# Two transformer blocks in one kernel: where the activation halves begin in SBUF, and the order of the first weight split

## The reference

```python
# block 1
h = rms_norm(x, g); proj = h @ w_in                  # 1024 -> 5120
o = stick_breaking_attention(q, k, v)                # 8 heads of 64
y_conv = (cb * causal_dwconv(cc * cx)) @ w_conv_branch
merged = sigmoid(g_att) * (o @ w_att_branch) + sigmoid(g_conv) * y_conv
x = x + rms_norm(merged @ w_out, g)
u = causal_dwconv(rms_norm(x, g) @ w_up)             # 1024 -> 2 * 2816
x = x + rms_norm((gelu(g) * a) @ w_down, g)          # 2816 -> 1024
# block 2
proj = rmsnorm(x, g) @ w_in_2                        # 1024 -> 9240
o_a = gated_delta_rule(...); o_b = forgetting_attention(...)
merged = sigmoid(gate_a) * (o_a @ w_proj_gdn) + sigmoid(gate_b) * (o_b @ w_proj_fox)
h = x + merged @ w_out_2
x = h + square(relu(rmsnorm(h, g) @ w_up_2)) @ w_down_2   # 1024 -> 4096 -> 1024
```

## Time and profile before

| | |
|---|---|
| median of three executions | 984.99 us |
| the profiled execution's own time | 984.24 us |
| its span, first to last instruction | 982.5 us |
| TensorE busy | 960.6 us (98%) |
| VectorE, ScalarE, GpSimd busy | 574.6, 510.4, 214.0 us |
| mean granted TensorE clock | 0.997 of full speed |
| HBM read | 150.20 MB, 154 GB/s over the span |
| the chain that ended last, by engine | PE 91%, DVE 4%, ACT 2%, others 1% or less |

### The profile page before, as it was taken

How to read it: one execution, slowest core, us unless ns; L and a number is a source line. 1 busy time by engine, 2 the same in 40 slices (tenths; PEclk the granted TensorE clock), 3 DMA queues, 4 the chain that set the end, 5 groups by cost and what they waited for, 6 DMA issues and landing times.

```text
span 982.5 us, 16651 instructions
## 1 busy us (share of the span) xinstructions
PE 960.6 (98%) x6923; PEld 885.9 (90%) x6923; DVE 574.6 (58%) x813; ACT 510.4 (52%) x764; POOL 214.0 (22%) x202
## 2 busy tenths in 40 slices
PE   7999999999999998999999989999999999999998
PEld 7998999799999887887899988999899989998886
DVE  5457556678788545664266785552555756454442
ACT  5475864566665344566556842323354456654331
POOL 6001003501111002257243772221100002210000
PEclk9999999999999999999999999999999999999999
DMA  8643455566564553335334423112145557666550
GB/s 273 235 142 108 147 176 193 155 215 205 184 212 173 192 193 129 129 129 172 129 127 131 134 83 129 44 43 87 51 165 180 172 164 215 181 206 209 176 193 22
DMA packets 125775, 152.32 MB, mean 155 GB/s; under 512 B 5105, under 2 KB 99588, under 8 KB 125700
## 3 DMA queue, kind: packets, MB, share of 16 engines
q1 hardware_dynamic: 125684, 151.25, 46.4%
q10 hardware_dynamic: 16, 0.00, 0.0%
HBM read 150.20 MB, written 1.05 MB: 154 GB/s over the span
## 4 chain that ended last, share of the span: by engine, by line
PE 91%; DVE 4%; ACT 2%; issue 1%; DMA 1%; POOL 1%; SPq 0%; DVEq 0%; POOLq 0%; ACTq 0%
PE ps L1790 77%; PE ps L1753 6%; PE ps L1987 4%; PE ps L1750 2%; DMA raw<-in_w_in 1%; DVE wl L775 1%; DVE gv L801 1%; PE ps L1967 0%; PE ps L1912 0%; ACT wh L1299 0%; DVE xres L801 0%; DVE tA L1038 0%; PE ps L1881 0%; DVE gq L1044 0%; POOL rs L553 0%
## 5 line engine op out<-in xcount | busy, mean ns | idle before, releaser
L775 DVE TENSOR_TENSOR wl<-raw,wh 128x1024 fp32r<-128x1024 f32 (+1 forms) x261 | 313.8, 1219 | 214.8 <-ACT wh L1299 214.5
L1790 PE MATMUL ps<-xh,wh 128*128 128x256 f32 x1280 | 362.5, 284 | 2.8 <-ACT wh L1299 2.4
L1790 PE MATMUL ps<-xh,wl 128*128 128x256 f32 x1280 | 355.9, 278 | 1.0 <-DVE wl L775 1.0
L1790 PE MATMUL ps<-xl,wh 128*128 128x256 f32 x1280 | 351.5, 277 | 0.0
L1299 ACT ACTIVATE wh<-raw 128x1024 fp32r<-128x1024 f32 (+1 forms) x292 | 286.8, 1023 | 120.3 <-PE ps L1790 117.1
L1790 PEld LDWEIGHTS ps<-xh,wh 128*128 128x128 f32 x1280 | 242.2, 189 | 7.0 <-issue 3.2
L1790 PEld LDWEIGHTS ps<-xh,wl 128*128 128x128 f32 x1280 | 241.7, 189 | 1.2 <-DVE wl L775 1.2
L1790 PEld LDWEIGHTS ps<-xl,wh 128*128 128x128 f32 x1280 | 239.1, 188 | 0.1
L561 POOL TENSOR_TENSOR wl<-raw,wh 128x1024 fp32r<-128x1024 f32 (+1 forms) x31 | 81.1, 2615 | 128.9 <-ACT wh L1299 126.9
L761 POOL TENSOR_TENSOR rr<-rr 128x512 f32<-128x512 f32 x16 | 16.7, 1042 | 159.9 <-ACT f2H L1741 159.9
L1790 PE MATMUL ps<-wl,f2H 128*128 128x512 f32 x128 | 50.5, 395 | 0.0
(11 more groups left out here) (349 smaller groups left out, 1495.6 us busy)
## 6 DMA issues: line engine op xcount, KB each, us to landing
raw<-in_w_in SPq DMA_DIRECT2D x56, 1024.0 KB, 4.8
raw<-in_w_up SPq DMA_DIRECT2D x38, 1024.0 KB, 5.3
raw<-in_w_down SPq DMA_DIRECT2D x26, 1024.0 KB, 4.8
raw<-in_w_out SPq DMA_DIRECT2D x8, 1024.0 KB, 4.9
raw<-in_w_proj_fox SPq DMA_DIRECT2D x4, 1024.0 KB, 4.9
raw<-in_w_proj_gdn SPq DMA_DIRECT2D x4, 1024.0 KB, 4.9
raw<-in_w_conv_branch SPq DMA_DIRECT2D x4, 512.0 KB, 3.4
raw<-in_w_att_branch SPq DMA_DIRECT2D x4, 512.0 KB, 3.3
```

The costliest lines, as they stand in the source:

```text
L775: e.tensor_tensor(L, R, H.bitcast(F32), ALU.subtract).then_inc(lo.sem)
L1790: k = e.matmul(o, l, r, start=opens, stop=done and n == ends[c], skip_group_check=True)
```

## The change

`STAYS` = 256 and `MOVES` = 192 replace the places. Moving activations (yc, o, ob, oa) go to 192, stationary ones (m1, f, m, f2) to 256; buffers that lie between them (gates, `ya`, `yg`, `rr`, `mt`) go along. `XH`, `XL` and the weights stay where they are. At the start, the DMA of `GP` is issued after the weights of units 0 to 2 and the small rows; ScalarE makes the first half of `WH` ahead of the first four `XH` chunks, and VectorE the first half of `WL` ahead of the first four `XL` chunks.

```diff
+STAYS, MOVES = 256, 192
...
-        assert base + R0 + 80 * KB + 384 <= nc.sbuf_usable_end, (base + R0 + 80 * KB, nc.sbuf_usable_end)
+        assert base + R0 + 80 * KB + STAYS <= nc.sbuf_usable_end, (base + R0 + 80 * KB, nc.sbuf_usable_end)
...
-        ycH = reg("ycH", [P, 4, T], 37, F32R, place=128)
-        oH = reg("oH", [P, 4, T], 45, F32R, place=320)
-        m1H = reg("m1H", [P, 8, T], 0, F32R, place=320)
-        fH = reg("fH", [P, FC1, T], 0, F32R, place=128)
-        ya = [reg(f"ya{i}", [P, 2, T], 44 + 2 * i, place=128) for i in range(2)]
-        obH = reg("obH", [P, 8, T], 60, F32R, place=384)
-        oaH = reg("oaH", [P, 8, T], 24, F32R)
-        mH = reg("mH", [P, 8, T], 0, F32R)
-        f2H = reg("f2H", [P, FC2, T], 0, F32R, place=384)
-        rr = [reg(f"rr{i}", [P, 2, T], 64 + 2 * i, place=384) for i in range(3)]
+        ycH = reg("ycH", [P, 4, T], 37, F32R, place=MOVES)
+        oH = reg("oH", [P, 4, T], 45, F32R, place=MOVES)
+        m1H = reg("m1H", [P, 8, T], 0, F32R, place=STAYS)
+        fH = reg("fH", [P, FC1, T], 0, F32R, place=STAYS)
+        ya = [reg(f"ya{i}", [P, 2, T], 44 + 2 * i, place=STAYS) for i in range(2)]
+        obH = reg("obH", [P, 8, T], 60, F32R, place=MOVES)
+        oaH = reg("oaH", [P, 8, T], 24, F32R, place=MOVES)
+        mH = reg("mH", [P, 8, T], 0, F32R, place=STAYS)
+        f2H = reg("f2H", [P, FC2, T], 0, F32R, place=STAYS)
+        rr = [reg(f"rr{i}", [P, 2, T], 64 + 2 * i, place=STAYS) for i in range(3)]
...
@@ sync @@
             for a in range(2):
                 e.dma_start(XRES[:, a, :], xv[:, a, :]).then_inc(ld_x[a], 16)
-            e.dma_start(GP[:], norm_mix_post[0].partition_broadcast(P)).then_inc(ld_gp, 16)
             for u in range(NRAW):
                 weights(u)
...
+            e.dma_start(GP[:], norm_mix_post[0].partition_broadcast(P)).then_inc(ld_gp, 16)
             for u in range(NRAW, U_UP + 3):
                 weights(u)
@@ vector @@
+            low(0, 0)
             for c in range(4):
                 x_low(0, CG["mix"], c)
-            low(0, 0)
             low(0, 1)
@@ scalar @@
                 squares(a)
+            high(0, 0)
             e.wait_ge(*cols("g0"))
             x_high(0, CG["mix"], 0)
             x_high(0, CG["mix"], 1)
-            high(0, 0)
             high(0, 1)
```

More of the change, by code:

```diff
@@ L142, in two_blocks @@
         att = [[reg(f"at{n}{i}", [P, 384], 25 + 1.5 * (2 * n + i)) for i in range(2)] for n in range(4)]
-        ycH = reg("ycH", [P, 4, T], 37, F32R, place=128)
-        ycL = reg("ycL", [P, 4, T], 41, F32R, place=128)
-        oH = reg("oH", [P, 4, T], 45, F32R, place=320)
[L146 to L150, removed]
-        m1H = reg("m1H", [P, 8, T], 0, F32R, place=320)
-        m1L = reg("m1L", [P, 8, T], 8, F32R, place=320)
-        fH = reg("fH", [P, FC1, T], 0, F32R, place=128)
-        fL = reg("fL", [P, FC1, T], 22, F32R, place=128)
-        ya = [reg(f"ya{i}", [P, 2, T], 44 + 2 * i, place=128) for i in range(2)]
-        yg = [reg(f"yg{i}", [P, 2, T], 48 + 2 * i, place=128) for i in range(2)]
+        ycH = reg("ycH", [P, 4, T], 37, F32R, place=MOVES)
+        ycL = reg("ycL", [P, 4, T], 41, F32R, place=MOVES)
+        oH = reg("oH", [P, 4, T], 45, F32R, place=MOVES)
+        oL = reg("oL", [P, 4, T], 49, F32R, place=MOVES)
+        sga = reg("sga", [P, 8, T], 53, place=MOVES)
+        sgc = [reg(f"sgc{i}", [P, 2, T], 61 + 2 * i, place=MOVES) for i in range(2)]
+        mcv = reg("mcv", [P, 8, T], 65, place=MOVES)
+        mt = [reg(f"mt{i}", [P, 2, T], 73 + 2 * i, place=MOVES) for i in range(2)]
+        m1H = reg("m1H", [P, 8, T], 0, F32R, place=STAYS)
+        m1L = reg("m1L", [P, 8, T], 8, F32R, place=STAYS)
+        fH = reg("fH", [P, FC1, T], 0, F32R, place=STAYS)
+        fL = reg("fL", [P, FC1, T], 22, F32R, place=STAYS)
+        ya = [reg(f"ya{i}", [P, 2, T], 44 + 2 * i, place=STAYS) for i in range(2)]
+        yg = [reg(f"yg{i}", [P, 2, T], 48 + 2 * i, place=STAYS) for i in range(2)]
         gsw = reg("gsw", [P, 8, 24], 76)
@@ L178, in two_blocks @@
         gst = reg("gst", [24, T], 59)
-        obH = reg("obH", [P, 8, T], 60, F32R, place=384)
-        obL = reg("obL", [P, 8, T], 68, F32R, place=384)
+        obH = reg("obH", [P, 8, T], 60, F32R, place=MOVES)
+        obL = reg("obL", [P, 8, T], 68, F32R, place=MOVES)
         Ev = FG[:].rearrange("p a (h t) -> p a h t", h=8)
@@ L196, in two_blocks @@
         oSv = FG[:].rearrange("p a (h d) -> p a h d", h=8)
-        oaH = reg("oaH", [P, 8, T], 24, F32R)
-        oaL = reg("oaL", [P, 8, T], 32, F32R)
-        mH = reg("mH", [P, 8, T], 0, F32R)
-        mL = reg("mL", [P, 8, T], 8, F32R)
-        sgb = [reg(f"sgb{i}", [P, 2, T], 76 + 2 * i, place=384) for i in range(2)]
-        f2H = reg("f2H", [P, FC2, T], 0, F32R, place=384)
-        f2L = reg("f2L", [P, FC2, T], 32, F32R, place=384)
-        rr = [reg(f"rr{i}", [P, 2, T], 64 + 2 * i, place=384) for i in range(3)]
+        oaH = reg("oaH", [P, 8, T], 24, F32R, place=MOVES)
+        oaL = reg("oaL", [P, 8, T], 32, F32R, place=MOVES)
+        mH = reg("mH", [P, 8, T], 0, F32R, place=STAYS)
+        mL = reg("mL", [P, 8, T], 8, F32R, place=STAYS)
+        sgb = [reg(f"sgb{i}", [P, 2, T], 76 + 2 * i, place=MOVES) for i in range(2)]
+        f2H = reg("f2H", [P, FC2, T], 0, F32R, place=STAYS)
+        f2L = reg("f2L", [P, FC2, T], 32, F32R, place=STAYS)
+        rr = [reg(f"rr{i}", [P, 2, T], 64 + 2 * i, place=STAYS) for i in range(3)]
         PS = [ctx.enter_context(nc.psum_tensor(f"ps{i}", [P, 512], F32)) for i in range(8)]
```

## The result

Seven executions of the changed kernel have a median of 976.99 us (975.13 to 982.75), seven of the kernel before 984.99 us (984.41 to 990.17). The ratio is 0.9914, with a 95% interval of [0.9889, 0.9939]. The first rival, both operands at 256 as a fast pair, had named 978.8 us and a chance of 0.20.

A forecast was written before the change was run, and what follows sets the result against it. TensorE's matmul stream was taken as the bound; -1.4 + 0.0 - 0.4 = -1.8 us on the profiled 984.24 gave 982.4, and 983.1 us for the median. The range was 978.6 to 988.0 us, the forecast's own about 980.5 to 985.

The forecast's parts named there:

- The first rival: Both operands at 256 are a fast pair: 512-column matmuls drop to 226.5 ns, 978.8 us in all; chance 0.20.
- What bounds the kernel: TensorE, with records for 98% of the span, sets the end; what is left to gain is its matmul stream's speed.
- Part 2: Stationary activations (m1, f, m, f2) to 256: pitch 231.8 ns, f and f2 -0.4, m1 -0.1, m +0.5, sum 0.0 us.
- Part 1: Moving activations to 192: o 0, oa -0.41, yc -0.30, ob -0.73, sum -1.4 us; attention gate's level left to the range.
- Part 3: The start: raw lands near 9.5 us, second half of WL at 14.8; +0.3 us at half clock, -1.1 at full, taken -0.4.
- The second rival: Long streams lock on the slow level: up projection at 117.8 ns costs 4.7 us, 987.8 us in all; chance 0.12.
- The third rival: Addresses do nothing and the levels have another cause; only the start gains 0.4 us, 984.6 us in all; chance 0.15.
- The sum: Parts 1 to 3 give -1.8 us; their ordinary extremes were said to give about 980.5 to 985 us.

The follow-up runs named there:

- the run of all pairs: Kernel with only TensorE's matmul streams, computation left out, at all 128 pairs of moving and stationary start addresses: 116.1 to 122.2 ns (256 columns), 231.3 to 237.1 ns (512).

## Why the prediction was wrong

- **What bounds the kernel** was right: the gain is in TensorE's stream, matmul by matmul.
- **Part 2 is the step that failed,** the pitch of the stationary activations at 256. The prediction says: "The nearest addresses on either side are 192 (233.4 and 228.7) and 320 (233.2); the fast one, 0, is the farthest away from 256." It took 231.8 ns, and 226.7 was measured: f and f2 -3.7 us instead of -0.4, m1 -0.2 instead of -0.1, and m kept its 226.7 ns where +0.5 us was expected. That is -3.9 us in place of 0.0. The pitch repeats every 256 bytes, as the run of all pairs shows, so the fast row of m (0 under 256) was the very pair that the change makes everywhere. The rows already held this: m at distance 256 was the odd one out, and f at 128 and f2 at 384, one class modulo 256, had the same pitch to 0.1 ns. I read them as a curve over 512 because the change was put in those terms. The first rival had the mechanism; its 978.8 us is 1.8 too high, because it shared the terms of parts 1 and 3, which were too small.
- **Part 1** had the direction and too small a size: -2.5 us (-1.6, -0.4 and -0.5) instead of -1.4. oa came out at -0.4, as forecast. The miss is the level of the attention gate and o. I let XH keep the slow level of before, but with yc at 192 nothing breaks the stream, and it keeps the fast level that it has from 119.20 on.
- **Part 3** was -2.2 us in the profiled execution against -0.4, more than its bound of -1.1 us at full clock. The mechanism (the clock decides) was right. The mis-sized term is the landing of raw: 8.5 us (8.50 to 9.11 in six profiles) instead of 9.5, so the whole chain through ScalarE and VectorE came 1.0 to 1.3 us earlier than I worked out: the second half of WL ended at 13.5 instead of 14.8. I took off GP's transfer alone, 1.4 us, and not its place in SyncE's queue: raw is issued at 1.69 us instead of 2.15. That is half of the missing microsecond; the rest stays open. The size is partly luck, since 15.40 is the earliest of the six new starts; the two in which the clock fell, 17.51 and 17.63, gain 0.1 us or nothing on the 17.62 of before, and 0.4 to 1.5 us on the other two old starts.
- **The second rival** is real, though not caused by the change: the up projection has one level in one execution and the other in the next (three of eleven profiles slow), 4.6 us apart, as worked out, and 12 of 29 executions of before were of the longer kind. It did not decide the median.
- **The third rival**, addresses that do nothing, is out: with the other engines idle the run of all pairs measures 116.1 to 122.2 ns in mode B by addresses alone. The Trainium skill, page "SBUF — State Buffer", section "Who interferes with whom", has two independent read ports for TensorE and says that it never waits on anyone. Of waiting for other engines no run here tells anything; for TensorE's own two operands the measurement decides against their being independent, since the pitch goes with the distance between them. What in the chip does it, no run shows.
- **The sum.** The extremes of the parts, as printed, add up to 979.8 to 985.2 us and not to 980.5 to 985. 976.99 lies below either.

What stays open: what picks the level when a stream sets in, what at the start decides whether the clock falls, and why mode B and mode A have opposite best distances.

## What to carry to other kernels

Where TensorE bounds a kernel, read the pitch of each steady stream over dozens of matmuls, and compare it between streams of one shape; here, steady differences of 2 to 6% were an address or a level, not noise. Before you interpolate between such readings, look for the period: two far-apart settings with equal values (128 and 384 here) name it. And split the executions by kind before comparing medians, since one stage whose level changes from execution to execution can hide or feign a change of half a per cent.

## What the runs showed of the hardware

- In fp32r streams of the high and low parts, a 512-column matmul has 226.7 ns where moving and stationary operand begin at the same address modulo 256 bytes, 232.4 ns at distance 128 and 233.2 ns at 192. A 256-column one reached 113.3 ns only at moving minus stationary = 192 modulo 256, and has 117.8 to 119.9 ns at the other multiples of 64.
- The 192 class of mode B has a second steady level, 117.8 ns. Which one a stream takes depends on how it sets in: two short matmuls ahead of it moved 378 matmuls from 117.8 to 113.3 ns, in both profiles that have them. In the up projection a level then held for over a thousand matmuls.
- An offset of 16 bytes from the best distance of mode B loses it entirely: all twelve streams at -80 and at -48 had 121.3 to 121.7 ns, against 116.0 to 116.4.
- The granted clock fell, or did not, in the same code: with raw landing at 8.50 to 8.86 us it stayed at full in four profiles, with 9.02 and 9.11 it fell to half in two, and 0.6 us of landing went with 2.2 us of start.
